# Where the split weights and the streamed tiles begin in SBUF: a fused two-layer trunk on one core

## The reference, cut to what matters

```python
for i in range(DEPTH):                      # 2 layers, x is (1, 256, 1024) float32
    x = x + 0.5 * swiglu(rmsnorm(x, norm_ff1[i]), ff1_w_gate[i], ff1_w_up[i], ff1_w_down[i])
    x = x + token_mixer(rmsnorm(x, norm_mix[i]), w_in[i], ...)   # two gated mixers, then w_out
    x = x + 0.5 * swiglu(rmsnorm(x, norm_ff2[i]), ff2_w_gate[i], ff2_w_up[i], ff2_w_down[i])
    g = jax.nn.sigmoid(rmsnorm(x, norm_ple[i]) @ ple_w_gate[i])
    x = x + g * (p[i] @ ple_w_proj[i])
return rmsnorm(x, norm_final)
```

## Time and profile before

| | |
|---|---|
| runs | 1181.15 and 1181.44 us, median 1181.3 |
| span of the profiled execution | 1179.5 us |
| TensorE matmuls, busy | 1168.9 us (99%), 10534 instructions |
| VectorE, ScalarE, GpSimd busy | 814.0, 593.7, 122.8 us |
| HBM read | 216.15 MB, 184 GB/s over the span |

### The profile page before, as it was taken

How to read it: one execution, slowest core, us unless ns; L and a number is a source line. 1 busy time by engine, 2 the same in 40 slices (tenths; PEclk the granted TensorE clock), 3 DMA queues, 4 the chain that set the end, 5 groups by cost and what they waited for, 6 DMA issues and landing times.

```text
span 1179.5 us, 24037 instructions
## 1 busy us (share of the span) xinstructions
PE 1168.9 (99%) x10534; PEld 1144.7 (97%) x10534; DVE 814.0 (69%) x939; ACT 593.7 (50%) x669; POOL 122.8 (10%) x136
## 2 busy tenths in 40 slices
PE   9999999999999999999999999999999999999997
PEld 9999999999999999999999999999899999999996
DVE  5866555688978766655786665558798777666455
ACT  5544445555745544444554444447367455444443
POOL 2000001011512000001210000100133020000011
PEclk9999999999999999999999999999999999999998
DMA  7655555545445555555555555554635365555541
GB/s 288 235 203 188 193 201 177 184 156 202 145 149 207 190 188 206 183 204 187 179 202 194 194 199 184 197 203 139 214 140 169 118 235 203 184 204 186 186 172 36
DMA packets 33384, 218.87 MB, mean 186 GB/s; under 512 B 5184, under 2 KB 6016, under 8 KB 7296
## 3 DMA queue, kind: packets, MB, share of 16 engines
q1 hardware_dynamic: 33280, 217.34, 53.2%
HBM read 216.15 MB, written 1.05 MB: 184 GB/s over the span
## 4 chain that ended last, share of the span: by engine, by line
PE 98%; DVE 1%; DMA 1%; ACT 0%; issue 0%; POOL 0%; SPq 0%; POOLq 0%; DVEq 0%
PE psum L385 31%; PE psum L387 31%; PE psum L386 31%; PE psum L665 1%; PE psum L644 1%; DMA x_all<-in_x 1%; PE psum L517 0%; PE psum L578 0%; PE psum L628 0%; PE psum L699 0%; PE psum L424 0%; PE psum L710 0%; PE psum L613 0%; DVE gates L1671 0%; PE psum L733 0%
## 5 line engine op out<-in xcount | busy, mean ns | idle before, releaser
L1222 DVE TENSOR_TENSOR w_lo<-raw,w_hi 128x2048 fp32r<-128x2048 f32 x200 | 457.9, 2293 | 213.5 <-ACT w_hi L856 213.4
L856 ACT ACTIVATE w_hi<-raw 128x2048 fp32r<-128x2048 f32 x201 | 385.2, 1917 | 366.6 <-PE psum L387 360.8
L385 PE MATMUL psum<-hA_hi,w_hi 128*128 128x256 f32 x1360 | 377.9, 278 | 0.0
L386 PE MATMUL psum<-hA_hi,w_lo 128*128 128x256 f32 x1360 | 375.7, 276 | 0.0
L387 PE MATMUL psum<-hA_lo,w_hi 128*128 128x256 f32 x1360 | 375.7, 276 | 0.0
L385 PEld LDWEIGHTS psum<-hA_hi,w_hi 128*128 128x128 f32 x1360 | 255.4, 188 | 2.7 <-issue 2.7
L386 PEld LDWEIGHTS psum<-hA_hi,w_lo 128*128 128x128 f32 x1360 | 255.4, 188 | 0.0
L387 PEld LDWEIGHTS psum<-hA_lo,w_hi 128*128 128x128 f32 x1360 | 255.3, 188 | 0.0
L385 PE MATMUL psum<-hB_hi,w_hi 128*128 128x256 f32 x832 | 230.3, 277 | 1.1 <-DVE w_lo L1654 1.1
L386 PE MATMUL psum<-hB_hi,w_lo 128*128 128x256 f32 x832 | 229.7, 276 | 0.0
L387 PE MATMUL psum<-hB_lo,w_hi 128*128 128x256 f32 x832 | 229.7, 276 | 0.0
(11 more groups left out here) (182 smaller groups left out, 1226.0 us busy)
## 6 DMA issues: line engine op xcount, KB each, us to landing
raw<-in_weights SPq DMA_DIRECT2D x203, 1024.0 KB, 4.9
raw<-in_weights SPq DMA_DIRECT2D x2, 512.0 KB, 6.2
out<-gates SPq DMA_DIRECT2D x3, 256.0 KB, 2.2
x_all<-in_x SPq DMA_DIRECT2D x1, 520.0 KB, 3.9
x_all<-in_x SPq DMA_DIRECT2D x1, 512.0 KB, 6.2
relu<-in_p SPq DMA_DIRECT2D x2, 256.0 KB, 5.0
consts<-in_consts SPq DMA_DIRECT2D x1, 384.0 KB, 5.7
out<-gates SPq DMA_DIRECT2D x2, 128.0 KB, 2.3
```

The lines of the kernel that those rows point to most:

```text
L385: pe.matmul(o, lh, rh, start=start, stop=False)
L386: pe.matmul(o, ll, rh, start=False, stop=False)
L856: act.activation(w_hi[:, s, :], raw[:, s, :], ACT.Copy).then_inc(hi_ready[s], 1)
L1222: dve.tensor_tensor(w_lo[:, s, :], raw[:, s, :], w_hi[:, s, :].bitcast(F32), ALU.subtract).then_inc(lo_ready[s], 1)
```

## The change

The high and low weights, two tiles with three slots each, become six tiles of their own. Each tile is 16 words longer than the chunk, and the chunk begins 12, 8 or 4 words into it for slot 0, 1 or 2: 48, 32 or 16 bytes past a multiple of 128, the same for the high and the low part of a slot. Behind each of the six stands a tile of 64 bytes, and six small tiles (`mean`, `rstd`, `r_eighth`, `r_less`, `r_half`, `gbias`) that stood further behind now live in these. The filler ahead of `hA` is computed anew and keeps `hA` at 64 bytes past a multiple of 512. `BEFORE_HB` grows by 16 words; with the six small tiles gone, `hB`, `hid` and the tiles of `mix` that share its space now begin 64 bytes past a multiple of 128 (320 past a multiple of 512). All other lines of the diff only write `w[s]` for `w[:, s, :]`. Instructions, order, waits, shapes and DMAs stay as they are.

```diff
-LO_PLACE = 128
+PLACES = (12, 8, 4)
 MOVING_PLACE = 192
-BEFORE_HB = 96
+BEFORE_HB = 112
...
-        w_hi = sb("w_hi", [P, SLOTS, 2048], F32R)
-        sb("before_w_lo", [P, LO_PLACE // 4])
-        w_lo = sb("w_lo", [P, SLOTS, 2048], F32R)
-        sb("before_hA", [P, (MOVING_PLACE - LO_PLACE) % 512 // 4])
+        w_hi, w_lo, between = [], [], []
+        for part, slots in (("hi", w_hi), ("lo", w_lo)):
+            for s in range(SLOTS):
+                slots.append(sb(f"w_{part}{s}", [P, 2048 + 16], F32R)[:, PLACES[s]:PLACES[s] + 2048])
+                between.append(sb(f"between_{part}{s}", [P, 16]))
+        mean, rstd, r_eighth, r_less, r_half, gbias = (t[:, 0:2] for t in between)
+        sb("before_hA", [P, (MOVING_PLACE - 2 * SLOTS * 128) % 512 // 4])
...
-        mean = sb("mean", [P, 2])
-        rstd = sb("rstd", [P, 2])
-        r_eighth = sb("r_eighth", [P, 2])
-        r_less = sb("r_less", [P, 2])
-        r_half = sb("r_half", [P, 2])
-        gbias = sb("gbias", [P, 2])
...
-                act.activation(w_hi[:, s, :], raw[:, s, :], ACT.Copy).then_inc(hi_ready[s], 1)
+                act.activation(w_hi[s][:, :], raw[:, s, :], ACT.Copy).then_inc(hi_ready[s], 1)
...
-                dve.tensor_tensor(w_lo[:, s, :], raw[:, s, :], w_hi[:, s, :].bitcast(F32), ALU.subtract).then_inc(lo_ready[s], 1)
+                dve.tensor_tensor(w_lo[s][:, :], raw[:, s, :], w_hi[s][:, :].bitcast(F32), ALU.subtract).then_inc(lo_ready[s], 1)
```

More of the change, by code:

```diff
@@ L389, in by_columns @@
             def by_columns(s, o, h, columns=(0, 1)):
-                wh, wl = (w[:, s, :].rearrange("p (k n) -> p k n", n=256) for w in (w_hi, w_lo))
+                wh, wl = (w[s][:, :].rearrange("p (k n) -> p k n", n=256) for w in (w_hi, w_lo))
                 for c in columns:
@@ L409, in by_tokens @@
             def by_tokens(s, o, h, ks, first, last, ahead=None):
-                wh, wl = (w[:, s, :].rearrange("p (k n) -> p k n", n=512) for w in (w_hi, w_lo))
+                wh, wl = (w[s][:, :].rearrange("p (k n) -> p k n", n=512) for w in (w_hi, w_lo))
                 for i, k in enumerate(ks):
@@ L480, in ffn @@
                     s = operands(L, off + DOWN + c)
-                    wh, wl = (w[:, s, :].rearrange("p (u n) -> p u n", n=256) for w in (w_hi, w_lo))
+                    wh, wl = (w[s][:, :].rearrange("p (u n) -> p u n", n=256) for w in (w_hi, w_lo))
                     for u in range(8):
@@ L534, in mix @@
                 wait_free(pe, L, "small")
-                wh, wl = (w[:, s, 0:1024].rearrange("p (k n) -> p k n", n=P) for w in (w_hi, w_lo))
+                wh, wl = (w[s][:, 0:1024].rearrange("p (k n) -> p k n", n=P) for w in (w_hi, w_lo))
                 for k in range(8):
@@ L797, in embed @@
                 pe.wait_ge(p_lo, L + 1)
-                wh, wl = (w[:, s, :].rearrange("p (k n) -> p k n", n=1024) for w in (w_hi, w_lo))
+                wh, wl = (w[s][:, :].rearrange("p (k n) -> p k n", n=1024) for w in (w_hi, w_lo))
                 for m in range(8):
@@ L886, in split_pieces @@
                 for i in range(4):
-                    act.activation(w_hi[:, s, piece(i)], raw[:, s, piece(i)], ACT.Copy).then_inc(piece_hi if i < 3 else hi_ready[s], 1)
+                    act.activation(w_hi[s][:, piece(i)], raw[:, s, piece(i)], ACT.Copy).then_inc(piece_hi if i < 3 else hi_ready[s], 1)
             def take_rb(L, k, b):
@@ L1112, in _ @@
                 for m in (2 * i, 2 * i + 1):
-                    act.activation(w_hi[:, 0, piece(m)], raw[:, 0, piece(m)], ACT.Copy).then_inc(piece_hi if m < 3 else hi_ready[0], 1)
+                    act.activation(w_hi[0][:, piece(m)], raw[:, 0, piece(m)], ACT.Copy).then_inc(piece_hi if m < 3 else hi_ready[0], 1)
             squares(0, 0, 0)
@@ L1116, in _ @@
             for i in range(4):
-                act.activation(w_hi[:, 1, piece(i)], raw[:, 1, piece(i)], ACT.Copy).then_inc(next_hi if i < 3 else hi_ready[1], 1)
+                act.activation(w_hi[1][:, piece(i)], raw[:, 1, piece(i)], ACT.Copy).then_inc(next_hi if i < 3 else hi_ready[1], 1)
                 if i == 1:
@@ L1235, in split_pieces @@
                         dve.wait_ge(hi_ready[s], t)
-                    dve.tensor_tensor(w_lo[:, s, piece(i)], raw[:, s, piece(i)], w_hi[:, s, piece(i)].bitcast(F32), ALU.subtract
+                    dve.tensor_tensor(w_lo[s][:, piece(i)], raw[:, s, piece(i)], w_hi[s][:, piece(i)].bitcast(F32), ALU.subtract
                                       ).then_inc(piece_lo if i < 3 else lo_ready[s], 1)
             def next_piece(i):
-                dve.tensor_tensor(w_lo[:, 1, piece(i)], raw[:, 1, piece(i)], w_hi[:, 1, piece(i)].bitcast(F32), ALU.subtract
+                dve.tensor_tensor(w_lo[1][:, piece(i)], raw[:, 1, piece(i)], w_hi[1][:, piece(i)].bitcast(F32), ALU.subtract
                                   ).then_inc(next_lo if i < 3 else lo_ready[1], 1)
@@ L1653, in _ @@
                         dve.wait_ge(hi_ready[0], 1)
-                    dve.tensor_tensor(w_lo[:, 0, piece(m)], raw[:, 0, piece(m)], w_hi[:, 0, piece(m)].bitcast(F32), ALU.subtract
+                    dve.tensor_tensor(w_lo[0][:, piece(m)], raw[:, 0, piece(m)], w_hi[0][:, piece(m)].bitcast(F32), ALU.subtract
                                       ).then_inc(piece_lo if m < 3 else lo_ready[0], 1)
```

## The result

The changed kernel takes 1225.3 us (two runs, 1225.30 and 1225.37) against 1181.3: a ratio of 1.037, interval 1.034 to 1.040. It is 44 us slower. The forecast was 1181, with 1148 to 1210 as its range; the rival "the step rises" had 1224 for all three slots.

The account below looks back on a forecast made before the run. TensorE's matmul-to-matmul step was taken as the bound: 9168 x 113.4 ns, 1039.7 us, 88% of the span. All changes were priced at 0, so 1181.3 + 0 = 1181 us, range 1148 to 1210.

Parts of the forecast that it names:

- the step rises: Rival: TensorE's 256-column matmuls keep 4.6 ns slower steps, 42 us, 1224 with three slots; chance 0.25 including VectorE as bound.
- TensorE's step: Time from one matmul to the next, 113.4 ns over 9168 matmuls; each nanosecond is worth 9.17 us.
- ScalarE, VectorE and the small tiles: Engine passes over the weights at new places, and short instructions reading moved two-word tiles: priced at 0.
- the price of the moving tiles: TensorE's streamed operands hB and hid begin 64 bytes further: claimed to cost and bring nothing, 0.
- the choice for the weights: Weights at 48, 32 and 16 bytes: bounds 1145 and 1224; took no change, as for the moving tiles.
- the hand-over in the earlier trace: Where hA hands over to hid without a break, steps stay 0.12 and 0.11 us; read as a free distance change.
- the slow steps of the earlier trace: Behind a break, 10 TensorE steps take 1.18 us, 118.0 ns each, with the same operands at the same places.
- the step falls: Rival: the new distance lets TensorE's two streams pass better; full price 1145, half 1157 to 1170; chance 0.33.
- the 109.5 of the transposes: Step in ns of TensorE's transposes, which load 128 fresh columns but stream only 128; at it products gain 36 us.
- The slot changes: Weights' place changes every 48 matmuls; might cost ten slow steps on each of about 205 chunks, 9 us; taken as nothing.

## Why the prediction was wrong

**The part that held.** TensorE's step was the only lever; 9168 matmuls at 9.17 us for each nanosecond is how the loss came, to within the reading of the steps (4.7 to 5.1 ns times 9.17 gives 43 to 47 us, measured 44.0). ScalarE, VectorE and the small tiles cost nothing, as summed. The granted clock stayed.

**The step that failed** is the price of the moving tiles, and with it the choice for the weights. I took the earlier trace rows for a comparison of two distances, 64 with `hA` and 0 with `hB` and `hid`, found equal steps, and carried "no change" from there to the steps of 16 bytes. But the distance was 64 in all three stretches: the rows were one case seen three times, and so was the hand-over in the earlier trace rows. The reason for the misreading is plain arithmetic, the lengths of six small tiles. When the comparison is really made, 64 bytes cost `hB` and `hid` 5.7 ns a step: the moving tiles, priced at 0, cost 25.6 us alone, and the weights' places, priced at 0 after them, 42.8 us alone. (The three steps were also equal only to 0.06 ns, 0.01 us in 178 steps, not to a hundredth of a nanosecond; that did no harm.)

**The rival that came true** was "the step rises", with its price: 118.0 ns a step and 42 us for three slots, 1224; measured 118.1 to 118.5 and 44.0, 1225.3. What spoke for it, the slow steps of the earlier trace rows, was the right row to weigh. What I set against it, that the rhythm stands with `hA` at 64 as with `hB` at 0, was the misread row again. Without it nothing in the trace of before spoke for the new places, so the chance of 0.12 for all three slots was too small for what was known. The prediction did write that the distances tried look "as if they were one case", but used it only for the rival of a gain.

**The rival "the step falls"** has no run behind it. Seventeen distances have now been run (0 to 16 and 48 to 80 mostly in steps of 4, and 32, 96 and 112), and no chunk's 256-column steps average less than 113.3 ns. None of these placings comes near the 109.5 of the transposes.

**The slot changes**, with 9 us above, are close to nothing in the changed kernel, where no fast step is left to lose; where every distance is a good one, slots that differ go with 2 to 3 us when the distance is 64, or 64 and 52 (1184.7 and 1183.4), and with nothing when it is 52 in all three, though the slots stand as far apart (1181.4).

**What the runs settle and what not.** Shown: the slow step comes from the distance between stationary and moving operand; two bad parts do not add; one bad load of the three is enough to lose the fast step. Read from traces, with no run that changes it alone: at 64 modulo 128, chunks stay slow only where the high weights are at 64 modulo 256. Not shown: by what inside the memory or TensorE a distance of 64, 52 or 76 lets the two reads pass and 48, 56, 60, 68 or 72 does not. That the two reads get in each other's way is the likely reading of the run in which both were moved together, but no run separates them in time.

The page "SBUF — State Buffer" of the Trainium skill, section "Who interferes with whom", gives TensorE two independent read ports and has it wait on no one; here the same instructions take 1181 or 1227 us by 4 bytes of distance between the two operands. What the prediction drew from the page, that the places cannot matter, does not hold in this kernel; the measurement decides.

## What to carry to other kernels

When matmuls with freshly loaded weights follow each other without a break, look at the step from start to start, not at the busy share, and treat the distance between the stationary and the moving operand as a tuned quantity: keep it at a value that was measured to be good in all products, and measure it again whenever anything in front of either tile changes its length. Take addresses from the built program before you call two stages a comparison. And if two parts of a change can each spoil the same thing, undoing one can bring almost nothing back (1224.0 for 1225.3 us).

## What was not expected of the hardware

- Four bytes more or less between the two operands of TensorE cost 3.9% of this kernel (1226.8 for 1180.9 us), and eight more bring all of it back (1181.4).
- At a good distance the fast step is a state that TensorE falls into, not a rate: the same stage of one kernel runs 86 matmuls in 10 us and then 91.
- The loss does not depend on how far the distance is off: at 0, 48, 56, 60 and 68 alike the mean step of `hA`, `hB` or `hid` in a slot lies between 117.6 and 119.8 ns.
